# Keys before values in a decoder layer's K/V stage: the order of weight blocks, norms applied as per-row scales, and a fourth cache slot

## The reference, cut to what matters

```python
def decoder_layer(x, c, lp, lam_init, attend):
    mod = (jax.nn.silu(c) @ lp["w_ada"] + lp["b_ada"]).reshape(B, 1, N_MOD, D_MODEL)
    h = rms_norm(x, lp["norm_ffn1"]) * (1.0 + sc1) + sh1
    x = x + 0.5 * g1 * swiglu(h, gate, up, down)
    h = rms_norm(x, lp["norm_mix"]) * (1.0 + sc2) + sh2
    q_a, k_a, v_a, q_b, k_b, v_b, g_a, g_b = jnp.split(h @ lp["w_in"], cuts, axis=-1)
    q_a, k_a, q_b, k_b = each rms_norm over its 64-wide heads, with a gain
    o_a, o_b = attend(q_a, k_a, v_a, q_b, k_b, v_b, lam)
    o_b = rms_norm(o_b, lp["subln_diff"]) * (1.0 - lam_init)
    mixed = (jax.nn.sigmoid(g_a) * (o_a @ w_branch_moba) + jax.nn.sigmoid(g_b) * (o_b @ w_branch_diff)) @ lp["w_out"]
    x = x + g2 * mixed
    h = rms_norm(x, lp["norm_ffn2"]) * (1.0 + sc3) + sh3
    x = x + 0.5 * g3 * swiglu(h, gate, up, down)
    rows = (k_a, v_a, k_b, v_b)      # the normed keys and the values are outputs too
```

## Time and profile before

| | |
|---|---|
| median of 3 runs | 780.7 us |
| the profiled execution | 779.16 us, of which the span 777.5 us |
| PE busy | 731.2 us, 94% |
| DVE busy | 481.4 us, 62% |
| ACT busy | 321.1 us, 41% |
| POOL busy | 124.0 us, 16% |
| moved by DMA | 209.53 MB, mean 270 GB/s |
| chain that ended last | PE 73%, DVE 15%, DMA 6%, issue 2%, ACT 2%, SPq 1% |

### The profile page before, as it was taken

How to read it: one execution, slowest core, us unless ns; L and a number is a source line. 1 busy time by engine, 2 the same in 40 slices (tenths; PEclk the granted TensorE clock), 3 DMA queues, 4 the chain that set the end, 5 groups by cost and what they waited for, 6 DMA issues and landing times.

```text
span 777.5 us, 16997 instructions
## 1 busy us (share of the span) xinstructions
PE 731.2 (94%) x6620; PEld 646.6 (83%) x6620; DVE 481.4 (62%) x692; ACT 321.1 (41%) x515; POOL 124.0 (16%) x179
## 2 busy tenths in 40 slices
PE   5899999999999998988878999999989999999997
PEld 2398988999998797867864666669979999999997
DVE  2664445454454998999988545678676555555441
ACT  1453333434343652333315443464544434434431
POOL 0000000002000303867863323210000000000000
PEclk9999999999999999999988999999999999999999
DMA  8978889888985855999999998995615655546530
GB/s 349 376 238 277 323 292 323 301 258 327 386 274 164 323 165 187 378 402 406 405 389 388 406 403 319 358 367 171 195 56 185 195 165 186 188 154 197 173 100 29
DMA packets 116520, 209.53 MB, mean 270 GB/s; under 512 B 6714, under 2 KB 100186, under 8 KB 104162
## 3 DMA queue, kind: packets, MB, share of 16 engines
q1 hardware_dynamic: 106784, 159.47, 59.5%
q0 software_dynamic: 9440, 49.02, 16.1%
q10 hardware_dynamic: 226, 0.10, 0.0%
HBM read 205.31 MB, written 3.24 MB: 268 GB/s over the span
## 4 chain that ended last, share of the span: by engine, by line
PE 73%; DVE 15%; DMA 6%; issue 2%; ACT 2%; SPq 1%; ACTq 0%; DVEq 0%
PE bank L1482 20%; PE bank L1483 19%; PE bank L1484 19%; DMA kvA<-in_cache_k_moba 4%; DMA early<-in_w_ada 3%; PE bank L1842 3%; PE bank L1538 2%; DVE kvA L1201 2%; DVE kvB L1201 2%; PE bank L1802 1%; DVE wlo L981 1%; PE bank L1803 1%; PE bank L1804 1%; DVE rstd L1181 1%; PE bank L1731 1%
## 5 line engine op out<-in xcount | busy, mean ns | idle before, releaser
L981 DVE TENSOR_TENSOR wlo<-raw,whi 128x1024 fp32r<-128x1024 f32 (+1 forms) x177 | 208.6, 1200 | 186.7 <-ACT whi L674 184.5
L1482 PE MATMUL bank<-hhi,whi 128*128 128x264 f32 x992 | 287.5, 290 | 5.7 <-DVE wlo L981 1.9
L1483 PE MATMUL bank<-hlo,whi 128*128 128x264 f32 x992 | 282.7, 285 | 0.0
L1484 PE MATMUL bank<-hhi,wlo 128*128 128x264 f32 x992 | 282.3, 285 | 0.0
L674 ACT ACTIVATE whi<-raw 128x1024 fp32r<-128x1024 f32 (+1 forms) x192 | 194.6, 1035 | 107.0 <-PE bank L1484 81.1
L1482 PEld LDWEIGHTS bank<-hhi,whi 128*128 128x128 f32 x992 | 188.3, 190 | 18.7 <-issue 15.0
L1483 PEld LDWEIGHTS bank<-hlo,whi 128*128 128x128 f32 x992 | 188.4, 190 | 0.2
L1484 PEld LDWEIGHTS bank<-hhi,wlo 128*128 128x128 f32 x992 | 187.6, 189 | 0.0
L1482 PE MATMUL bank<-ahi,whi 128*128 128x264 f32 x416 | 119.6, 288 | 0.4 <-DVE alo L1440 0.4
L1484 PE MATMUL bank<-ahi,wlo 128*128 128x264 f32 x416 | 118.1, 284 | 0.0
L1483 PE MATMUL bank<-alo,whi 128*128 128x264 f32 x416 | 117.8, 283 | 0.0
(11 more groups left out here) (258 smaller groups left out, 811.6 us busy)
## 6 DMA issues: line engine op xcount, KB each, us to landing
raw<-in_ffn_w_gate SPq DMA_DIRECT2D x22, 1024.0 KB, 5.4
raw<-in_ffn_w_up SPq DMA_DIRECT2D x22, 1024.0 KB, 5.8
raw<-in_w_ada SPq DMA_DIRECT2D x20, 1024.0 KB, 6.9
raw<-in_w_in SPq DMA_DIRECT2D x20, 1024.0 KB, 10.9
raw<-in_ffn_w_down SPq DMA_DIRECT2D x16, 1024.0 KB, 5.6
kvB<-in_cache_k_diff POOLq DMA_DIRECT2D x44, 256.0 KB, 6.4
kvA<-in_cache_k_moba SPq DMA_DIRECT2D x44, 256.0 KB, 7.7
kvA<-in_cache_v_moba SPq DMA_DIRECT2D x44, 256.0 KB, 6.6
```

What stands on the lines that cost most here:

```text
L981: dve.tensor_tensor(half_view(wlo[key[1] % 2], key, t), half_view(raw[s], key, t), half_view(whi[key[1] % 2], key, t).bitcast(F32), ALU.su ...
L1482: mm(out, wh, xh, start=start, stop=False)
L1483: mm(out, wh, xl, start=False, stop=False)
L1484: return mm(out, wl, xh, start=False, stop=stop)
```

## The change

1. `KV_BLOCKS` becomes k0 k1 k2 k3 v0 v1 v2 v3.
2. The q heads are no longer normed over their full width. Of the sample columns (8 per chunk) the root is taken and `qT` is scaled (`sample_q_norm`). For the prompt the sums of squares are kept by token, `qroot` holds root and reciprocal, and the factor goes into the softmax: the bias is multiplied by slope times root, the exponential gets the reciprocal as its scale. The gain goes into ScalarE's copy.
3. K halves: squares are summed by token (three matmuls with the two-column `half` as moving operand), ScalarE applies the reciprocal root as a per-partition scale when it copies the turned keys to `ktok`, and TensorE turns them back for `kT` (`k_back`, `k_final`).
4. Each cache gets a slot more for use 0 alone, `kv_first`, at `vtok` (A) and `gT` (B); it waits for the held modulation products. Use u >= 4 still waits for use u-3.
5. `scores(ab, u)` is called for one cache: A's use u+2 and B's use u in step u, A's uses 0 and 1 ahead of the K/V products. `replicate_q`, `place_q`, `turn_keys` and the semaphore `s_qrow` are split by cache.
6. The first sample softmax half moves to steps 10 to 16; `AHEAD`, `K_ROWS` and `V_ROWS` follow the new order. POOL's low halves are issued beside use g instead of use g-2.

The core of the diff:

```diff
-KV_BLOCKS = [("k", 0), ("v", 0), ("k", 1), ("k", 2), ("k", 3), ("v", 1), ("v", 2), ("v", 3)]
+KV_BLOCKS = [(kind, i) for kind in "kv" for i in range(4)]
...
         def kv_slot(ab, use):
-            if use % KVS < KVS - 1:
-                return kv[ab][use % KVS]
-            return kv_lent[ab]
+            if use == 0:
+                return kv_first[ab]
+            return kv[ab][(use - 1) % KVS] if (use - 1) % KVS < KVS - 1 else kv_lent[ab]
...
+            if use == 0:
+                eng.wait_ge(s_ada, ADA_N2 + 4)
-            if use == KVS - 1:
+            if use == KVS:
...
-            if 0 <= prev < 16:
+            if 1 <= prev < 16:
                 eng.wait_ge(s_kS[ab], prev + 1)
...
-        AHEAD = {4: [W_KV + 5], 6: [W_KV + 6], 8: [W_KV + 7], 10: [W_GATE], 12: [W_GATE + 1], 14: [W_GATE + 2],
-                 18: [W_GATE + 3, W_GATE + 4], 19: [W_GATE + 5], 21: [W_GATE + 6], 23: [W_GATE + 7], 25: [W_BR]}
+        AHEAD = {5: [W_KV + 4], 8: [W_KV + 5], 10: [W_KV + 6], 12: [W_KV + 7], 14: [W_GATE], 16: [W_GATE + 1],
+                 18: [W_GATE + 2, W_GATE + 3, W_GATE + 4], 19: [W_GATE + 5], 21: [W_GATE + 6], 23: [W_GATE + 7], 25: [W_BR]}
...
-            for use in range(KVS - 1):
+            for use in range(KVS):
                 kv_load(sp, 0, use)
             load_w(W_KV + 1)
             load_w(W_KV + 2)
-            kv_load(sp, 0, KVS - 1)
+            kv_load(sp, 0, KVS)
             load_w(W_KV + 3)
-            load_w(W_KV + 4)
-            for use in range(KVS, 4 * TS):
+            for use in range(KVS + 1, 4 * TS):
...
-                if use + 2 < POOL_HALVES:
-                    lo(*filler(use + 2))
+                if 5 <= use < POOL_HALVES - 1:
+                    lo(*filler(use))
+                if use == POOL_HALVES - 2:
+                    lo(*filler(use + 1))
...
-                nc.scalar.activation(rstd[:, i % 2, :], bank[:, 4, 0:T], ACT.Sqrt, bias=C("eps"), scale=1.0 / 64).then_inc(s_kroot, 1)
+                for rows_, c0, c1 in ((P, 0, 4), (TS, 4, 6)):
+                    ins = nc.scalar.activation(kroot[0:rows_, i, c0:c1], bank[0:rows_, 4, 8 * i + c0:8 * i + c1], ACT.Sqrt, ...)
...
+            def k_tokens(g, i):
+                a.wait_ge(s_turn, i + 1)
+                a.wait_ge(s_krecip, i + 1)
+                for tt in range(2):
+                    for h in range(2):
+                        ins = nc.scalar.activation(ktok[:, tt, e0:e0 + 64], bank[:, g % 4, d0:d0 + 64], ACT.Copy, scale=kroot[:, i, q:q + 1])
+                ...
+            def k_final(i):
+                a.wait_ge(s_kback, i + 1)
+                nc.scalar.activation(kT[:, i, :], bank[:, 5, 0:T], ACT.Copy).then_inc(s_knorm, 1)
...
-                    nc.scalar.activation(plog[h][:, 0:128], plog[h][:, 0:128], ACT.Exp, bias=stat[:, o + 3:o + 4], accum_out=stat[:, o + 5:o + 6])
+                    nc.scalar.activation(plog[h][:, 0:128], plog[h][:, 0:128], ACT.Exp, bias=stat[:, o + 3:o + 4], scale=qroot[:, 2, j:j + 1],
+                                         accum_out=stat[:, o + 5:o + 6])
...
-                dve.reciprocal(rstd[:, i % 2, :], rstd[:, i % 2, :]).then_inc(s_krecip, 1)
-                v.wait_ge(s_krecip, i + 1)
-                dve.scalar_tensor_tensor(out=kT[:, i, :], in0=kT[:, i, :], scalar=misc[:, g:g + 1], in1=rstd[:, i % 2, :], ...)
+                dve.reciprocal(kroot[:, i, 0:4], kroot[:, i, 0:4])
+                dve.reciprocal(kroot[0:TS, i, 4:6], kroot[0:TS, i, 4:6]).then_inc(s_krecip, 1)
...
-                    ch.link(dve.scalar_tensor_tensor(out=plog[h][:, :], in0=C("dist"), scalar=-slope_of_row(j), in1=bank[:, h, 0:384], ...))
+                    for tb, (e0, e1) in enumerate(((0, 128), (128, 384))):
+                        q = 16 * tb + j
+                        ins = dve.scalar_tensor_tensor(out=plog[h][:, e0:e1], in0=C("dist", e0, e1), scalar=qroot[:, 1, q:q + 1], in1=bank[:, h, e0:e1],
+                                                       op0=ALU.mult, op1=ALU.add)
...
+            def k_back(i):
+                pe.wait_ge(s_tok, 2 * (i + 1))
+                ...
+                for tt in range(2):
+                    nc.tensor.transpose(bank[:, 5, P * tt:P * tt + P], ktok[:, tt, f0:f0 + 128], ident)
+                nc.tensor.transpose(bank[:, 5, TP:T], ktoks[:, f0:f0 + 128], ident[0:TS, 0:TS]).then_inc(s_kback, 1)
...
             def head_sum(u):
-                for t in range(2):
-                    ins = mm(bank[:, 6 + t, 0:T], C("blockdiag"), sqb[:, t, :], start=True, stop=True)
+                pe.wait_ge(s_qsq, u + 1)
+                mm(bank[:, 7, 16 * u:16 * u + 16].rearrange("p (t s) -> p t s", s=TS), C("blockdiag"), sqb[:, :, TP:T], start=True, stop=True)
+                for t in range(2):
+                    for tb in range(2):
+                        ins = mm(bank[:, 7, c0:c0 + 2], sqb[:, t, P * tb:P * tb + P], C("half"), start=True, stop=True)
...
+            scores(0, 0)
+            head_sum(3)
+            scores(0, 1)
+            replicate_q(1)
...
-            for u in range(2 * TS + 2):
-                if u <= 2:
-                    kv_product(u)
-                if 2 <= u < 16:
-                    kv_product(u + 1)
+            for u in range(2 * TS + 1):
+                kv_product(u)
 ...
-                if u >= 2:
-                    scores(u - 2)
+                if u + 2 < 16:
+                    scores(0, u + 2)
+                if u < 16:
+                    scores(1, u)
```

More of the change, by code:

```diff
@@ L603, in _ @@
             pool.wait_ge(s_ptab, 16)
-            for use in range(KVS):
+            for use in range(KVS + 1):
                 kv_load(pool, 1, use)
@@ L1196, in turn_keys, with sample_q_norm @@
-            def turn_keys(u):
-                for ab in range(2):
-                    slot = kv_slot(ab, u)[:, :, :].rearrange("p q d -> p (q d)")
-                    v.wait_ge(s_kv[ab][u % KVS], kv_landed(u))
-                    dve.transpose(slot, slot).then_inc(s_kT[ab], 1)
-            def place_q(s):
+            def sample_q_norm(ab):
+                v.wait_ge(s_nvar, ab + 1)
+                root = qnorm[:, 32 * ab:32 * ab + 32]
+                ch.link(dve.reciprocal(root, root))
+                v.wait_ge(s_proj, 2 * ab + 2)
+                dst = qT[:, 4 * ab:4 * ab + 4, TP:T]
+                dve.tensor_tensor(dst, dst, root.rearrange("p (c s) -> p c s", s=TS), ALU.mult).then_inc(s_qk, 1)
@@ L1681, in k_turn @@
+            def k_turn(g, i):
+                pe.wait_ge(s_kproj, i + 1)
+                b = g % 4
+                for tt in range(2):
+                    nc.tensor.transpose(bank[:, b, P * tt:P * tt + P], kT[:, i, P * tt:P * tt + P], ident)
+                nc.tensor.transpose(bank[0:TS, b, 256:384], kT[:, i, TP:T], ident).then_inc(s_turn, 1)
+            def k_back(i):
+                pe.wait_ge(s_tok, 2 * (i + 1))
                 if i:
-                    pe.wait_ge(s_tok, 2 * i)
+                    pe.wait_ge(s_knorm, i)
@@ new lines, in scores @@
+            def scores(ab, u):
+                s, half = divmod(u, 2)
+                b6, c0 = 6 + s // 4, 256 * (s // 2 % 2) + 128 * half
+                if half == 0:
+                    pe.wait_ge(s_qrow[ab], s + 1)
+                pe.wait_ge(s_kT[ab], u + 1)
+                for b in range(4):
+                    for m in range(4):
+                        ins = mm(bank[32 * m:32 * m + 32, b6, c0:c0 + 128].rearrange("p (q c) -> p q c", q=4), qrow[s % 2][:, 16 * ab + 4 * m + b, :],
+                                 kv_slot(ab, u)[:, :, 128 * m + 32 * b:128 * m + 32 * b + 32],
+                                 start=(u % 8 == 0 and ab == 0 and b == 0), stop=(u % 8 == 7 and ab == 1 and b == 3))
+                ins.then_inc(s_kS[ab], 1)
```

291 lines of the change are left out of this document (155 added, 136 removed).

## The result

The changed kernel takes 776.89 us (median of 6 runs, 774.0 to 779.77) against 781.82 us for the one before (6 runs, 779.87 to 783.59): a ratio of 0.9946, 95% interval 0.9923 to 0.997; by the ratio that is 4.2 us. Ten further runs of it, made later beside the experiments, gave 778.87 us and 0.9971 (0.9945 to 0.9996), by the ratio 2.3 us. Both intervals exclude no change; together they reach from 0.3 to 6 us. I had forecast 773.0, a gain of 7.7: the sign was right, the size was two to three times what came in the runs. The profiled execution has a span of 773.6 us (777.5 before), 3.9 less.

The account below looks back on a forecast made before the run. DVE and the transfers were taken to bound the key stage. Product 19 9.1 us earlier, value loop +1.0, handshakes 0.4 back: -7.7 us, predicting 773.0 us, range 768 to 779.

Parts of the forecast that it names:

- Start of the caches: Blocks 0 wait for the last held modulation product until 256.6 us, 5 us later than before; costed at nothing.
- product 0: First K/V product on PE, behind 6.4 us of head sums, scores and replications: starts at 290.0 us instead of 283.6.
- 3 units ahead: By 313 us in the key stage, cache and weight transfers are 3 units of 1.05 MB ahead, some 8 us.
- PE's sum: PE's key-stage work until block 15 of cache B is scored: 94.5 us without waits, ending at 384.5 us.
- DVE no longer bounds: Key stage: DVE loses 34.9 us and gains 5, net 30 less; a key step holds some 5.3 us.
- The sign that I had named: Profile sign: DVE under 0.85 busy in the key stage, with gaps released by DMA.
- The first softmax lies inside this stage and hides behind it: First softmax (exp sums, scale) lies in the key stage and was taken to hide behind it.
- The transfers' bound of 387.4: Key stage: 28.6 MB left at 400 to 406 GB/s land by 384 us; transpose and score give 387.4.
- Clock: PE's lower clock at 390.6 to 394 us, costing about 2.9 us, goes away; this is inside the 9.1 us.
- Value loop: 412 to 510 us, PE-bound: biased logits as two instructions cost +1.0 us (0 to +2.4); rescaling in the exponential free.
- Transfers stay the bound: Rival, chance 0.15: key stage still needs 6.6 to 7.0 us of transfer per step; gain 3, at most 5 us: 776 to 779.
- The turn back: Rival, chance 0.08: PE's key turn back waits for ACT and DVE behind landings over 14.7 us; 787 at 20 us.

Follow-up runs that it names:

- fourth-block run: Changed kernel with the fourth block of each cache asked for only when block 1 of cache A has been scored; ratio to the kernel before 1.0064.
- both other chains thinned: Changed kernel with half of each key page unread from block 4 on and the first softmax thinned on DVE; ratio to the kernel before 0.9822.
- thinned softmax: Changed kernel without ranking of the first half's blocks, own products as 4 operations writing zeros on DVE; ratio to the kernel before 0.9934.
- half the bytes: Changed kernel loading only half of each key page for blocks 4 to 15 of both caches; ratio to the kernel before 0.9914.
- GpSimd thinned: Changed kernel with GpSimd's low halves of the weight blocks cut to an eighth; ratio to the kernel before 0.9951.

## Why the forecast had the right sign and twice the size

- **Start of the caches, product 0, first steps: right.** Blocks 0 were asked for at 255.7, the fourth block of A at 273.8 and the fifth at 287.5 (289 forecast); product 0 began at 287.7 (290.0); DMA moved 239 GB/s between 286 and 302. My 3 units ahead, some 8 us of transfer, are what the fourth-block run prices: 5.9 us at product 19.
- **PE's sum: right and a little high.** A K step took 6.30 us, not 6.6. With both other chains thinned block 15 was scored at 381.4; my 384.5 had 2.3 us of it in a product 0 that came sooner.
- **"DVE no longer bounds": wrong, the step that failed.** I took 34.9 us off, 5 on, and divided the rest over steps of 5.3 us. From 256 to 412 us DVE's busy time fell by 18.8 (146.9 to 128.1), not 30: the second half's ranks now fall in the stretch, and operations held by POOL add some 9 (1.9 + 2.0 for the two above, 2.7 for the diagonal, 1.3 for q rows, 1.0 for own products). The new small operations themselves took 3.5 us, less than my 5. The sign that I had named came true all the same: from 312 to 386 us DVE is busy 62.34 of 74 us, 0.84, with gaps released by DMA. It could not tell a DVE that no longer bounds from one that bounds late. More important, an average over the stage was the wrong question. DVE stood idle 13.9 us early on for landings and then had turns and a softmax in order before the last block. "The first softmax lies inside this stage and hides behind it" failed with it: on PE it is hidden, on DVE it stands in front of a turn, for 3.1 us at product 19 by the traces with the thinned softmax, and for more where the transfers are lighter (401.2 with half the bytes, 396.6 with both: 4.6 us).
- **The transfers' bound of 387.4: right as a number, but not alone.** With the softmax thinned block 15 is scored at 388.2 and product 19 ends at 403.3, close to my 388 and 402.9. In the kernel as it is, landings and DVE's queue add up: 391.7 and 406.4. That is 3.5 of the missing 3.8 us of the spans' difference; the loop's 0.7 over my 1.0 adds to it, and the 0.4 that I took back for handshakes comes off. That the agreement is to 0.4 us is partly luck, given what executions differ by.
- **Clock: right at 390, wrong before.** From 390 to 394 the granted clock is 1.00, as forecast. But PE's waits of 2.5 and 3.3 us at 357 and 369 dropped it to half, scores taking 1.93 us and one product 3.98 between them.
- **Value loop: +1.7 instead of +1.0.** The mechanism was named, the exponentials were not in it: their second operand costs 0.09 us each, where I had put nothing. The two loops are not at one clock, either. From 412 to 460 us it is 0.93 before and 0.96 after; 0.07 and 0.04 of 48 us are, as an estimate, 3.4 and 1.9 us of lost clock, so at equal clocks the loop may have grown by up to 1.5 us more.
- **The rivals.** "Transfers stay the bound" gave 776 to 779 and the runs fell in it, but not by its reason alone: half the bytes bring product 19 to 401.2 only, and both edits to 396.6. The turn back never held PE (no wait on it in the table). The landings in the chain took 13 us, under the 14.7 from which I had it bite.

What stays open: why cache A's landings on SP's queue take 8.6 us in the median and 13 at worst while B's on POOL's take 6.7 (a weight block of 1 MB stands between them on SP, but that was not tried alone), and what decides how often a small operation meets one of POOL's.

## What to carry to other kernels

Taking work off an engine helps only if the work that it does in order before the last due item gets shorter; read which instructions stand in its queue between the last landing and the last turn, not its busy share. Where a round trip (slot free, transfer, turn, use) and an engine's queue are both near the bound, thin each alone and both together before forecasting: here 5.2 and 3.1 us became 9.8. And a slot that lets transfers start 14 us sooner or more was worth more (5.9 us at product 19, taken away from the changed kernel) than 23 us of one engine's time (1.4, given to the kernel before). Before reading a few us out of one trace, look how far two executions of the same stage lie apart: here 4 to 5 us.

## What the runs showed of the hardware that I had not expected

A gap of about 1.1 us on PE, the wait of its first products of the loop's second half for ACT, is in every trace of a kernel with the change (0.65 us with the value loop's additions taken back; in the kernel before it is 0.5). After it the granted clock stays full in some executions and falls in others. The changed kernel from the last work before the gap, and the run with the late fourth block at the same place (stretch, length, busy, PEclk, DMA share, GB/s):

```profile
459.00:468.00 9.00, 7.92 (x69) 5.83 (x72) 4.37 (x12) 3.80 (x9) 2.07 (x4) 1.00 0.79 296
```

```profile
465.00:474.00 9.00, 7.90 (x46) 4.57 (x47) 4.32 (x12) 3.61 (x8) 0.46 (x1) 0.68 0.68 264
474.00:480.00 6.00, 6.00 (x47) 3.96 (x46) 0.00 (x0) 1.11 (x4) 2.01 (x5) 0.92 0.90 306
```

In the same kind of nine microseconds PE gets through 69 matmuls at 1.00 and 46 at 0.68. The same products behind the gap take 3.8 us there, 5.1 with GpSimd thinned, 5.4 with the value loop's additions taken back, 5.9 with the fourth block late; with the gate product behind them the loss is nothing, 1.6 or 3.2 us. PE's instructions before the gap are the same in all of these; what tells the executions apart the traces don't show. So 1 to 3 us gained ahead of such a place can come or go there: in the profiled executions with GpSimd and with the softmax thinned the clock fell there (0.66 from 460 to 465 us in both), and their loops are 1.5 us longer, against 1.9 and 3.1 us gained at product 19. That the medians stayed where they were for the same reason is likely, but not shown.
